# A two-block transformer kernel on one core: scan prologue among the value projections, gate weights in the last scan step, and norm, queries and scores by token tile

## The reference, cut to what matters

```python
zx = split(modulate(rmsnorm(x, norm1_g), ...) @ w_in)        # attention inputs, zx[3] (3328 wide) for the scan, zx[4] gates
o_ax = diff_post(diff_attention(qx, k_all, v_all, lam), ...)
z = centred_shift(zx[3], shift_w)                            # r, k, v, wd, ad, gd
w_log = -softplus(-(w0 + tanh(wd) @ w_up)) - 0.5;  decay = exp(-exp(w_log))
a = sigmoid(a0 + ad @ a_up);  kk = head_l2norm(k * k_k);  k_eff = k * (1 + (a - 1) * k_a)
s = s * w - (s @ kk) (kk * a) + v k;  y = s @ r              # per token, two directions, 16 heads of 64 x 64
x = x + mod * ((g_a * (o_ax @ w_branch_a) + g_b * (o_bx @ w_branch_b)) @ w_out)
h = modulate(rmsnorm(x, norm2_g), ...)
q = h @ peer_wq;  s = q . peer_keys;  top 16 of 128 keys twice, top 16 of their 256 pairs -> eidx   # 8 heads
x = x + mod * sum_k gate_k * gelu(peer_u[eidx_k] . h) * peer_v[eidx_k]
```

## Time and profile before

| quantity | value |
|---|---|
| three executions | 2931.26, 2942.15, 6875.59 us |
| median | 2942.15 us |
| the profiled execution | 2937.36 us |
| its span, first to last instruction | 2935.4 us |
| mean granted TensorE clock | 0.953 |
| TensorE busy | 2653.9 us, 90% |
| VectorE busy | 1306.9 us, 45% |
| ScalarE busy | 611.1 us, 21% |
| GpSimd busy | 488.6 us, 17% |
| chain that ended last | TensorE 52%, issue 21%, DMA 13%, VectorE 6% |

### The profile page before, as it was taken

One profiled execution on the slowest core, in us unless ns is written; L12 is line 12 of the kernel. 1 busy time (PEld: TensorE's weight loads), 2 busy tenths in 40 slices (PEclk: granted clock), 3 DMA queues, 4 the chain that ended last, 5 costly groups with the idle time before them and its releaser, 6 DMA issues.

```text
span 2935.4 us, 54254 instructions
## 1 busy us (share of the span) xinstructions
PE 2653.9 (90%) x23428; PEld 1824.5 (62%) x23428; DVE 1306.9 (45%) x2837; ACT 611.1 (21%) x1330; POOL 488.6 (17%) x392
## 2 busy tenths in 40 slices
PE   8999999999999999999995988888999887887877
PEld 6688784568878533445885887887877433333333
DVE  2873210176431011354454444444213877777654
ACT  1242000114310001133223444332001111111111
POOL 0000000000000000000004433331001454544552
PEclk9999999999999999999996999999999899889899
DMA  5323333442333444223110000001334899999996
GB/s 193 144 93 138 142 145 143 159 153 93 115 144 151 165 172 186 86 108 151 72 43 1 2 2 2 2 2 53 142 137 173 363 421 421 421 421 422 421 421 286
DMA packets 55056, 507.00 MB, mean 173 GB/s; under 512 B 6112, under 2 KB 6112, under 8 KB 7520
## 3 DMA queue, kind: packets, MB, share of 16 engines
q0 software_dynamic: 37056, 269.12, 22.1%
q1 hardware_dynamic: 17824, 235.41, 21.0%
HBM read 503.46 MB, written 1.05 MB: 172 GB/s over the span
## 4 chain that ended last, share of the span: by engine, by line
PE 52%; issue 21%; DMA 13%; DVE 6%; PEld 4%; ACT 2%; DVEq 1%; POOL 1%; ACTq 0%; POOLq 0%; PEldq 0%
PE psum L1519 30%; PE psum L517 16%; DMA mem<-weights,mem 12%; PEld psum L1519 4%; PE psum L1954 4%; DVE mem L2720 2%; DVE mem L2243 2%; PE psum L744 1%; PE psum L533 1%; POOL mem L2850 0%; DMA mem<-vectors 0%; PE psum L1529 0%; DVE mem L2499 0%; ACT mem L2098 0%; DVEq L2518 0%
## 5 line engine op out<-in xcount | busy, mean ns | idle before, releaser
L1519 PE MATMUL psum<-mem 64*64 64x64 f32 (+6 forms) x17432 | 1053.5, 262 | 111.6 <-DVEq L2518 19.2
L1519 PEld LDWEIGHTS psum<-mem 64*64 64x64 f32 (+3 forms) x17432 | 814.1, 150 | 346.5 <-issue 219.8
L517 PE MATMUL psum<-mem 128*128 128x256 f32 (+9 forms) x4228 | 968.3, 399 | 4.2 <-ACTq L801 2.1
L517 PEld LDWEIGHTS psum<-mem 128*128 128x128 f32 (+4 forms) x4228 | 707.6, 183 | 257.3 <-issue 168.8
L1954 PE MATMUL psum<-mem 128*128 128x512 f32 x1024 | 506.5, 654 | 133.6 <-ACT mem L2226 133.4
L1954 PEld LDWEIGHTS psum<-mem 128*128 128x128 f32 x1024 | 210.0, 210 | 429.5 <-issue 250.4
L2850 POOL DMA_INDIRECT mem<-weights,mem x256 | 310.1, 1211 | 588.9 <-PE psum L1954 292.5
L2720 DVE CUSTOM_DVE_ANT_0 mem<-mem 128x1024 f32<-128x1024 f32 x256 | 308.1, 1225 | 143.4 <-DMA mem<-weights,mem 137.8
L2243 DVE TENSOR_TENSOR mem<-psum,mem 128x512 f32<-128x512 f32 (+1 forms) x224 | 150.9, 685 | 313.9 <-PE psum L1519 296.0
L2772 POOL TENSOR_TENSOR mem<-mem 128x512 f32<-128x512 f32 (+1 forms) x112 | 160.5, 1450 | 730.5 <-ACT mem L2075 470.2
L2243 DVE TENSOR_TENSOR mem<-mem 128x512 f32<-128x512 f32 (+4 forms) x200 | 144.6, 731 | 103.6 <-ACTq L2011 82.7
(11 more groups left out here) (228 smaller groups left out, 1306.9 us busy)
## 6 DMA issues: line engine op xcount, KB each, us to landing
mem<-weights SPq DMA_DIRECT2D x102, 2048.0 KB, 7.3
mem<-weights SPq DMA_DIRECT2D x2, 2176.0 KB, 8.3
mem<-weights,mem POOLq DMA_INDIRECT x256, 22.4
mem<-weights SPq DMA_DIRECT2D x2, 1536.0 KB, 7.8
mem<-weights SPq DMA_DIRECT2D x3, 1024.0 KB, 9.2
mem<-weights SPq DMA_DIRECT2D x2, 1152.0 KB, 8.6
mem<-weights SPq DMA_DIRECT2D x2, 1120.0 KB, 4.9
mem<-x SPq DMA_DIRECT2D x1, 1024.0 KB, 6.0
```

The source lines that it names most:

```text
L517: ins = pe.matmul(out, lhsT, rhs, start=start, stop=stop, skip_group_check=skip)
L1519: ins = pe.matmul(out, lhsT, rhs, start=start, stop=stop, skip_group_check=skip)
```

## The change

Three things are changed.

1. The prologue of scan step 0 moves among the value chunks. The items of the first two rw groups are cut in halves so that the slots of the last items are others. TensorE makes the rates of step 0 behind value chunk (4, 0), ScalarE and VectorE do their parts behind given chunks (`p` counts them), GpSimd starts when TensorE begins the last value item. The load of `lora`, the weights of the rates, is issued before item rw2. `scan_ready` is gone; the last shift is waited for in front of the values' product. The scan's tensors change places, `restart` has a copy for step 0, and the late half of `kk` is copied to its place by GpSimd within step 0.
2. The first gate item behind the scan is loaded after the last left matrix of step 7 instead of behind the scan; the second still waits for `scan_done`.
3. The merge goes bank by bank. `out2` goes token tile by token tile; the norm, the transposes and the modulation are made by tile (ScalarE takes tile 0, VectorE tile 1), and the first query item is multiplied by tile, so that the scores of tile 0 and the first two heads come before the rest of the queries.

The diff, cut to its core:

```diff
-RW_ITEMS = (0, 1, 2, 3, 6, 4, 5)
+RW_ITEMS = ((0, 0, 2), (0, 2, 2), (1, 0, 2), (1, 2, 2), (2, 0, 4), (3, 0, 4), (6, 0, 2), (4, 0, 4), (5, 0, 4))
...
-    r0, r1, r2, r3, Pm, nU, Rm, ARm, U0, Qm, Km, Dm, DTm, VT_TOK, Kt, Qt, Apk, Ark, Arq, LT, St = Z
+    r0, r1, r2, r3, Pm, Qm, Km, nU, Rm, ARm, U0, Dm, DTm, VT_TOK, Kt, Qt, Apk, LT, St, Ark, Arq = Z
...
+            if name == "rw2_0":
+                sp.wait_ge(*shift_parts_ready.at(0, 0))
+                sp.dma_start(lora, W2[:, w2_total:w2_total + 2048]).then_inc(lora_landed, 16)
             if n == LAST_BEFORE_SCAN + 1:
-
-                sp.wait_ge(shift_parts_ready.sem, 1)
-                sp.dma_start(lora, W2[:, w2_total:w2_total + 2048]).then_inc(lora_landed, 16)
-
+                sp.wait_ge(*lt_ready.at(7, 1))
+            if n == LAST_BEFORE_SCAN + 2:
                 sp.wait_ge(scan_done, 2)
...
+        for i, at, n in RW_ITEMS:
+            w = km_view(item(f"rw{i}_{at}"), P * n)
+            for c in range(at, at + n):
+                rw_chunk(w, i, c, at)
                 if (i, c) == (3, 1):
                     kk_sums(0)
                 if (i, c) == (6, 1):
                     kk_sums(1)
-            if i == 0:
+                if (i, c) == (4, 0):
+                    pe.wait_ge(lora_landed, 16)
+                    pe.wait_ge(*lora_act_ready.at(0))
+                    for d in range(2):
+                        rates(0, d)
...
-        pe.wait_ge(lora_landed, 16)
-        pe.wait_ge(*scan_ready.at(0))
...
+            if h == 0:
+                pe.wait_ge(*shift_parts_used.at(0, len(RW_ORDER) - 1))
...
+        def tile_transposes(t):
+            pe.wait_ge(*xn2_ready.at(0, 1 + t))
+            for q in range(2):
+                transposes((act_ring, dve_ring)[t], "hT", [xn[:, t, (4 * q + c) * P:(4 * q + c + 1) * P] for c in range(4)])
+
+        w = [km_view(item(f"out{half}"), 512) for half in range(2)]
+        for t in range(TT):
+            for half in range(2):
+                if (t, half) == (1, 1):
+                    tile_transposes(0)
+                b = dve_ring.open(pe, "out2")
+                for k in range(8):
+                    last = pe.matmul(b, mg2[:, k, t * P:(t + 1) * P], w[half][:, k, :], start=k == 0, stop=k == 7)
+                    if k == 0 and t == half:
+                        last.then_inc(weights.used, 1)
+                last.then_inc(dve_ring.full, 1)
...
+        def first_queries(b, t, chunks):
+            for c in chunks:
+                for k in range(8):
+                    last = mm(b[:, c * P:(c + 1) * P], w[:, k, c * P:(c + 1) * P], hT[:, k, t * P:(t + 1) * P], k == 0, k == 7)
+            return last
...
+        pe.wait_ge(*hT2_by_act.at(0, 2))
+        w = km_view(item("wq0"), 512)
+        b = act_ring.open(pe, "qp")
+        first_queries(b, 0, (0, 1))
+        tile_transposes(1)
+        first_queries(b, 0, (2, 3)).then_inc(act_ring.full, 1)
+        scored = act_ring.open(pe, "sp")
+        b = act_ring.open(pe, "qp")
+        pe.wait_ge(*hT2_by_dve.at(0, 2))
+        first_queries(b, 1, (0, 1))
+        pe.wait_ge(keys_landed, 16)
+        pe.wait_ge(*qTp_ready.at(0, 0))
+        score_products(scored, 0, 0)
+        first_queries(b, 1, (2, 3)).then_inc(act_ring.full, 1)
         h2_transposes(0)
-        pe.wait_ge(keys_landed, 16)
-        key_scores(0)
+        key_scores(0, (1,))
         h2_transposes(1)
...
-            if p == 19:
                 act.wait_ge(*shift_parts_used.at(0, RW_ORDER.index(24)))
                 A(zwa[0:64, :], zwa[0:64, :], ACT.Tanh).then_inc(lora_act_ready.sem, 1)
+            if p == 19:
+                sigmoids(0)
+            if p == 21:
+                first_decays(0)
+                removal_decays()
+                key_decays()
...
+        tile_root(0)
+        for q in range(2):
+            b = take("hT")
+            for c in range(4):
+                k = 4 * q + c
+                last = A(hT[:, k, 0:P], b[:, c * P:(c + 1) * P], ACT.Identity, bias=AB[:, 5, k:k + 1], scale=AB[:, 4, k:k + 1])
+            done(last)
+        act.drain().then_inc(hT2_by_act.sem, 1)
+        tile_root(1)
...
+        first_queries(0)
+        key_scores(0, (0,))
+        first_queries(1)
         h2_copies(0)
-        key_scores(0)
+        key_scores(0, (1,))
         h2_copies(1)
...
+                tt(kk_late, kk_late, Z_sq[:, 4:8, :], ALU.mult)
+                v.tensor_scalar(ka_rest, V2["k_a"], -1.0, 1.0, ALU.mult, ALU.add)
+                v.drain().then_inc(kk_ready.sem, 1)
+            if p == 18:
+                rate_sums()
+                restarts(first_restart)
+            if p == 19:
+                v.wait_ge(*rates_ready.at(0))
+                cumulate(0, first_restart)
+                cumulate(1, first_restart)
+            if p == 20:
+                exclude()
+            if p == 22:
+                chunk_decay(0)
+            if p == 23:
+                v.memset(yb, 0.0)
+                v.memset(St, 0.0)
+        v.drain().then_inc(state_ready.sem, 1)
...
+            if h == 0:
+                restarts(restart)
...
+                g, merged = gsig2[:, c:c + 2, :], mg2[:, c:c + 2, :]
+                done(tt(g if m else merged, b, g, ALU.mult))
+                if m:
+                    v.drain()
+                    tt(merged, merged, g, ALU.add)
+            v.drain().then_inc((gate2_used, merged2_ready)[m].sem, 1)
...
+                xs, y = x[:, t, cols_], xn[:, t, cols_]
+                done(tt(y, take("out2"), rows2[:, 0, cols_], ALU.mult))
                 v.drain()
-            v.sem_inc((gate2_used, merged2_ready)[m].sem, 1)
-        for half in range(2):
-            for t in range(TT):
-                xs, r = x[:, t, half * 512:(half + 1) * 512], rows2[:, 0, half * 512:(half + 1) * 512]
-                j = junk[:, (2 * half + t) * 512:(2 * half + t + 1) * 512]
-                done(tt(j, take("out2"), r, ALU.mult))
+                tt(xs, xs, y, ALU.add)
                 v.drain()
-                tt(xs, xs, j, ALU.add)
-        v.drain()
-        model_norm(1, x, xn)
-        normed_evac(2, hT)
+                v.tensor_tensor_reduce(y, xs, xs, 1.0, 0.0, ALU.mult, ALU.add, crs2[:, half:half + 1])
+            v.drain()
+            tt(css2[:, t:t + 1], crs2[:, 0:1], crs2[:, 1:2], ALU.add)
+            v.drain().then_inc(sumsq2_ready.sem, 1)
+            v.wait_ge(*root2_ready.at(0, 1 + t))
+            v.reciprocal(crs2[:, 0:1], csd2[:, t:t + 1])
+            v.drain()
+            v.tensor_scalar(xn[:, t, :], x[:, t, :], crs2[:, 0:1], None, ALU.mult)
+            v.drain().then_inc(xn2_ready.sem, 1)
...
+            else:
+                pool.wait_ge(*lt_ready.at(0, 0))
...
-        pool.wait_ge(*scan_ready.at(0))
+        pool.wait_ge(*kk_ready.at(0))
         pool.wait_ge(*rates_ready.at(0))
+        pool.wait_ge(weights.used, used0 + SLOTS + LAST_BEFORE_SCAN + 1)
...
+                pool.tensor_copy(kk[:, 4:8, :], kk_late)
+                pool.drain()
```

More of the change, by code:

```diff
@@ L1332, in build_program @@
     rb(256)
-    RW_ORDER = [4 * i + j for i in RW_ITEMS for j in range(4 if i < 6 else 2)]
+    RW_ORDER = [4 * i + at + j for i, at, n in RW_ITEMS for j in range(n)]
     slots_at = 2 * TT * D
@@ L1636, in _, with rw_chunk @@
                 modulation(7 + 2 * grp)
[L1638 removed]
+        def rw_chunk(w, i, c, at):
             b = act_ring.open(pe, "rw")
@@ L1841, in inverse @@
                     two.then_inc(inverseT_full.sem, 1)
-        for d in range(2):
-            rates(0, d)
         for h in STEPS:
```

204 lines of the change are left out of this document (97 added, 107 removed).

## The result

The changed kernel takes 2890.36 us (median of 4 runs, 2889.51 to 2895.87); the kernel before, in 4 runs beside it, 2948.02. The slow execution of before, 6875.59 us, counts in that median and not in the ratio; the other three took 2931.26, 2942.15 and 2953.89. The ratio is 0.9831 with a 95% interval of 0.9803 to 0.9859: about 1.7% less time. That is a gain clear of nothing, but within the 2% that counts as no change here, and it is at the predicted 2890. The profiled execution took 2895.87 us, the slowest of its four, with a span of 2894.1: 41.3 less than the span of before. From 2942.15 to the median of the changed kernel it is 51.8; the profile shows less partly because its execution was the slowest, and the three of before lie 23 us apart.

What follows compares the result with a forecast made beforehand. TensorE bounds most stretches through waits and its lower clock, DMA the expert gathers at the end. Gains of 25.2 + 10.3 + 12 = 47.5 us from the profiled 2937.36 give 2890 us, range 2874 to 2904.

Steps and rivals of the forecast that it cites:

- Part A: Scan prologue moved under the value projections: rates of step 1 start 25.2 us earlier, bounds 23 to 28.5.
- its cover: Scan prologue: GpSimd's products end at 1544 against the last value chunk's 1552, leaving 8 us to spare.
- (4): Value projections: rates drop TensorE to 1.2 GHz and it stays there, seven chunks cost 58 us; 2948 us, chance 0.03.
- (5): Scan start: the prologue stays last because an operand is released only at the end; 2915 us, chance 0.04.
- The row speaks against it: First rates: the profile row's 0.50 clock, at 7.09 of 7.20 us busy, overrules full clock and a chunk end at 1548.9.
- Part B: Gate weights loaded in the last scan step: TensorE's 7.90 us wait and 2.7 us of lower clock go; gain 10.3.
- Part C: Tail by token tiles: 15.9 us of idle and clock loss shrink to 3.7; gain 12, bounds 8.5 to 13.
- Who waits for it: Tail: the ninth gather needs the last query bank; the stream behind it is DMA-bound, so the end moves by 12.
- held by something other than the last queries: Sign of being wrong, at the gathers: something else than the last query bank holds them; no size given.
- (1): The clock falls to its lower level at every new seam, gains together 39; 2898 us, chance 0.15.
- (3): The tail keeps its end since gathers are DMA-bound, only Part A and Part B count; 2902 us, chance 0.07.
- (2): The clock helps: larger gains in all three parts and two more scan steps faster, 58 us; 2879 us, chance 0.10.

Runs made afterwards that it cites:

- rates_later: Changed kernel with the first rates, and the ScalarE and VectorE steps that follow them, one value chunk later; 2879.16 us, ratio 0.9794.
- gap_apart: rates_later with the wait for the rates' four banks put back one chunk earlier, behind chunk 18, a gap without small matmuls behind it; 2902.64 us, ratio 0.9855.
- ninth_late: Changed kernel with gathers nine to eleven waiting for the last scores instead of the last queries; 2893.0 us.
- fifteenth_late: Changed kernel with gathers 15 to 17 waiting for the sum of row 4 instead of rows 1, 2 and 3; 2895.1 us.
- c_alone: Kernel before with only the new tail (Part C); 2932.4 us, ratio 0.9960.
- no_c: Changed kernel with merge, norm, output projection, first queries and scores in the old order; 2901.9 us, ratio 0.9867.
- old_order: Changed kernel, but TensorE waits for token tile 1 at once, then computes the queries of item 0 over both tiles; 2900.14 us, ratio 0.9865.
- no_a: Changed kernel with the prologue of scan step 0 back behind the last value chunk; 2919.9 us, ratio 0.9932.

## Why the prediction was right

The time, 2890, is the predicted one, and the three terms stand in the trace near their sizes. One step of the reasoning was wrong all the same, without cost here, and one reading of a row. That the figure is met to the microsecond is luck: the prediction took 47.5 from the one profiled execution of before, 4.8 us below the 2942.15 in the middle of the others, and from there to the changed median it is 51.8.

- **Part A, forecast 25.2: 24.6 at the rates of step 1, 25.1 at their sigmoid.** Step by step from R: the last chunk's end was put at 67.0, the copy behind it starts at 67.8; 10.4 from there to the rates, measured 78.05 - 67.83 = 10.2. GpSimd was to start 39.3 us behind R, and started at 40.8; its cover was to be 8, and was 7.2. The second pair of rates did wait for the reciprocals, 2.67 us, and the clock was paid. So neither rival (4) nor (5) happened: the clock was back within the chunk, and the prologue ended under the value projections.
- **The reading of the clock was wrong in its cause.** The prediction took the 0.50 of the earlier trace rows as a property of the small matmuls, since TensorE was busy 7.09 of 7.20 us. But 9.90 us of idle stood right ahead of that row. rates_later shows the same matmuls between two chunks at 1.00, and gap_apart shows chunk matmuls at 0.50 behind a gap. The Trainium skill (TensorE: Matmul & The Clock Gate, Part 1) lets the clock follow how busy the array has lately been; these runs agree, and the sentence "The row speaks against it" read the engine's state in the row and not what it did before. The sum came out because the gap was in it, and with the gap the clock. By that rule the last chunk was to end 3.3 us earlier than forecast; with the rates one chunk later it ended 7.0 us earlier, since the wait went too.
- **Part B, forecast 10.3: 10.3.** From Y to the first mixing bank it was 58.5 us and is 48.2. No DMA wait, gate banks 6.9 apart, and neither the second gate item nor the output normalisation came last.
- **Part C, forecast 12 within 8.5 to 13: 13.8.** Last mixing bank to last query copy, 106.8 before and 92.9 after. The mechanism was as told; what was left was mis-sized. The gap of the merge was put at 1.7 and is 1.60; that of tile 1's norm at 1.1 and is 0.46; of the 0.9 for weight loads and a ring wait some 0.6 shows (the queries of item 0 in columns of 128 took about 14.4 us, the score product among them taken off, where two banks are 13.8). The loss to the clock doesn't show: it read 1.00 throughout from 2148 to 2188, although TensorE stood 1.60 us.
- **Who waits for it: the step that failed.** "From the ninth on the stream is bound by DMA, so the end moves by the same 12." ninth_late moved the ninth by 4.08 and the end by nothing; fifteenth_late moved the fifteenth by 5.01 and the end by 4.94. The prediction had named this among its signs of being wrong: gathers "held by something other than the last queries". The chain runs over scores, ranking and the first weighing. The number came right all the same, which no step of the prediction had secured, because parts B and C move the last queries, the scores of item 1 and so both gathers alike: the distance from the ninth to the fifteenth is 16.0 before and 16.2 after.
- **The rivals.** (1), (3), (4) and (5) didn't happen: every undone part costs its own amount in the end. Of (2) a part did: C above its estimate and a scan at a better clock, 3.4 us in the profile.
- **The sum.** 24.6 + 10.3 + 13.8 = 48.7 against 47.5. The spans differ by 41.3: R came 8.0 later in the execution after, the scan from step 1 on to Y took 3.4 less (28.48 between R and Y less 25.06), and from the fifteenth gather to the end it was 3.3 more (635.68 against 632.43). 8.0 - 25.1 - 3.4 - 10.3 - 13.8 + 3.3 = -41.3. The largest term of what is left over, the 8.0, is no part of the change: R lay anywhere from 1485 to 1494 in the fourteen profiles, early and late ones among kernels with and without part A (1493.79 in c_alone). The 3.4 of the scan is within its scatter (last section). The 3.3 behind the fifteenth gather are not explained.

## What to carry to other kernels

When a wait is removed, follow the whole chain to the resource that is short at the end, here DMA, and ask which transfer the stream truly hangs on: the first that found an empty queue in front of it and was never caught up with. An idle bracket before a transfer is not it when another follows whose end hangs on something else, here on VectorE's ranking. And price a gap on TensorE together with the clock behind it: a wait of 2.7 us cost 6 to 7 here, and moving its work by one chunk of 6.9 us gave all of it back.

## What the runs showed of the hardware

- **Gaps and the clock.** The granted clock fell to 0.50 in or just behind gaps of 2.67 us (eight kernels), 3.20 (before and no_c), 4.07 (old_order), 4.71 (gap_apart) and behind the longer ones (6.14, 7.77, 9.90). In old_order the eight transposes behind the gap still took 1.06 us, as at the full clock, and the level fell behind them, ahead of a second gap of 2.35. That a gap of 2.67 in an otherwise full stretch costs more in clock (3.3 to 4.3 us) than in idle time was not expected.
- **The length of the gap is not all.** Across the 1.60 us ahead of the output projection the clock stayed at 1.00 in all twelve kernels that have it. Ahead of the value projections TensorE stands only 1.4 us, between matmuls of 128 columns, and there the lower level followed in ten of the fourteen profiles and not in the other four. The changed kernel and no_a, behind that gap:

```profile
1406.00:1408.00 2.00, 2.00 (x10) 1.61 (x9) 1.54 (x4) 1.89 (x5) 0.00 (x0) 0.50 0.00 0
```

```profile
1399.00:1401.00 2.00, 1.34 (x9) 0.90 (x9) 1.85 (x5) 1.68 (x5) 0.00 (x0) 1.00 0.00 0
```

  What decides it is not shown by these runs.
- **The clock in the scan is not the same in every execution.** The stretch from 1575 to 1780 us is nearly the same part of the program in these two kernels (rates_later, gap_apart; no edit touches it), and the granted clock differs:

```profile
1575.00:1780.00 205.00, 181.90 (x6869) 173.12 (x6861) 100.58 (x138) 94.12 (x131) 86.93 (x61) 0.98 0.01 2
```

```profile
1575.00:1780.00 205.00, 185.16 (x6724) 176.30 (x6722) 92.91 (x131) 89.64 (x127) 81.90 (x63) 0.92 0.01 2
```

  Each of the four steps behind the sigmoid of step 1 took from 50.7 to 55.5 us, and the four together from 205.7 (no_a) to 219.6 (c_alone). Every step has waits of 1 to 2 us on TensorE. Whether the clock falls in them was not tied to anything in the kernels, and stays open. Over whole executions the time goes with the clock: of eleven executions of before beside rates_later the fastest took 2924.70 us at a mean granted clock of 0.963, the slowest 2952.32 at 0.945. That the scan holds most of this is likely, but only one execution of each kernel has a profile, so it is not shown.
- **VectorE beside GpSimd.** The shifts of the value chunks (three operands, 510 columns) took 0.75 us each while GpSimd was still. Beside its products (1533.9 to 1553.8) the six of them took from 1.02 to 2.68, and 0.75 again behind them:

```profile
1528.51 0.75 DVE L2504 SCALAR_TENSOR_TENSOR mem<-mem 128x510 f32<-128x510 f32 x1
...
1542.60 2.68 DVE L2504 SCALAR_TENSOR_TENSOR mem<-mem 128x510 f32<-128x510 f32 x1
```

  The Trainium skill (SBUF — State Buffer, Who interferes with whom) says that a VectorE instruction with two inputs in SBUF contends with a GpSimd instruction that reads SBUF; the trace agrees. It cost nothing here: the slowest pair took 3.7 us, and a chunk leaves VectorE 6.9.
